# A two-layer streaming encoder step: the layer loop unrolled, the norms crossed in two groups of 280 tokens, more weight slots

## The reference

```python
def _rmsnorm(x, g):
    xf = x.astype(jnp.float32)
    y = xf * lax.rsqrt(jnp.mean(xf * xf, axis=-1, keepdims=True) + EPS)
    return (y * g.astype(jnp.float32)).astype(x.dtype)
...
    h = _rmsnorm(x, p['g_pre_mix'])
    (qn, qr, ckv, kr, qb, kb, vb, qc, kc, vc, alr, gc, gate) = _split_cols(h @ p['w_in'])
    # A: latent attention, B: sliding-window attention, C: gated linear attention
...
def _merge(oa, ob, oc, gate, p):
    g = jax.nn.sigmoid(gate).reshape(gate.shape[:-1] + (N_BRANCH, D_MODEL))
    y = (g[..., 0, :] * (oa @ p['w_up_a']) + g[..., 1, :] * (ob @ p['w_up_b'])
         + g[..., 2, :] * (oc @ p['w_up_c']))
    return y @ p['w_out']

def _residual(x, mix, p):
    x = x + _rmsnorm(mix, p['g_post_mix'])
    f = jnp.square(jax.nn.relu(_rmsnorm(x, p['g_pre_mlp']) @ p['w_ff1'])) @ p['w_ff2']
    return x + _rmsnorm(f, p['g_post_mlp'])
```

## Time and profile before

| | |
|---|---|
| median of three runs | 2607.6 us |
| profiled execution | 2612.26 us |
| its span, first to last instruction | 2610.5 us |
| mean granted TensorE clock | 0.971 of full |
| busy: PE, PEld, POOL, DVE, ACT | 2465.8, 2280.5, 1123.3, 984.5, 943.5 us |
| loaded weight units | 305 of 512 KB |
| DMA | 189.45 MB, mean 73 GB/s |

### The profile page before, as it was taken

One profiled execution on the slowest core, in us unless ns is written; L12 is line 12 of the kernel. 1 busy time (PEld: TensorE's weight loads), 2 busy tenths in 40 slices (PEclk: granted clock), 3 DMA queues, 4 the chain that ended last, 5 costly groups with the idle time before them and its releaser, 6 DMA issues.

```text
span 2610.5 us, 42794 instructions
## 1 busy us (share of the span) xinstructions
PE 2465.8 (94%) x17996; PEld 2280.5 (87%) x17996; DVE 984.5 (38%) x1746; ACT 943.5 (36%) x1757; POOL 1123.3 (43%) x677
## 2 busy tenths in 40 slices
PE   7999999999999799999879999999999997999997
PEld 6999878798798799999779998878977997999996
DVE  4566435435622411111355555444256124111113
ACT  4344423332444432322334443333333544322322
POOL 5433223333355464544343432233334455645543
PEclk8999999999999899999989999999999998999998
DMA  4111311121123122222121114111211231222222
GB/s 149 56 63 55 105 54 49 45 69 56 41 73 116 42 88 89 82 89 82 64 81 57 62 56 118 41 49 47 75 49 41 81 108 49 82 89 86 85 90 84
DMA packets 57464, 189.45 MB, mean 73 GB/s; under 512 B 8048, under 2 KB 12880, under 8 KB 56624
## 3 DMA queue, kind: packets, MB, share of 16 engines
q1 hardware_dynamic: 47120, 165.90, 19.5%
q10 hardware_dynamic: 10144, 20.73, 2.5%
HBM read 172.44 MB, written 10.89 MB: 70 GB/s over the span
## 4 chain that ended last, share of the span: by engine, by line
PE 44%; DVE 3%; POOL 2%; ACT 1%; issue 1%; DVEq 0%; POOLq 0%
PE dense L695 35%; PE att L743 1%; PE att L930 1%; PE att L991 1%; DVE h_raw L1530 1%; PE att L881 1%; PE att L820 1%; POOL h_lo L1860 1%; PE att L806 0%; POOL wlo L1855 0%; DVE x L1513 0%; PE att L947 0%; PE att L964 0%; PE att L824 0%; PE att L997 0%
## 5 line engine op out<-in xcount | busy, mean ns | idle before, releaser
L1855 POOL TENSOR_TENSOR wlo<-wraw,whi 128x1024 fp32r<-128x1024 f32 x298 | 715.4, 2402 | 947.5 <-ACT whi L1060 947.5
L695 PE MATMUL dense<-h_hi,whi 128*128 128x280 f32 x3200 | 947.4, 296 | 17.5 <-ACT cproj L1098 8.3
L695 PE MATMUL dense<-h_lo,whi 128*128 128x280 f32 x3200 | 938.8, 293 | 0.0
L695 PE MATMUL dense<-h_hi,wlo 128*128 128x280 f32 x3200 | 936.6, 293 | 0.0
L695 PEld LDWEIGHTS dense<-h_hi,whi 128*128 128x128 f32 x3200 | 607.5, 190 | 41.3 <-issue 16.4
L695 PEld LDWEIGHTS dense<-h_hi,wlo 128*128 128x128 f32 x3200 | 606.4, 189 | 1.5 <-issue 0.8
L695 PEld LDWEIGHTS dense<-h_lo,whi 128*128 128x128 f32 x3200 | 607.0, 190 | 0.0
L1060 ACT ACTIVATE whi<-wraw 128x1024 fp32r<-128x1024 f32 x298 | 312.5, 1049 | 294.6 <-DMA wraw<-in_w 256.0
L695 PE MATMUL dense<-hid_lo,whi 128*128 128x280 f32 x1024 | 298.4, 291 | 0.0
L695 PE MATMUL dense<-hid_hi,whi 128*128 128x280 f32 x1024 | 297.8, 291 | 0.0
L695 PE MATMUL dense<-hid_hi,wlo 128*128 128x280 f32 x1024 | 297.6, 291 | 0.0
(11 more groups left out here) (290 smaller groups left out, 3619.5 us busy)
## 6 DMA issues: line engine op xcount, KB each, us to landing
wraw<-in_w SPq DMA_DIRECT2D x305, 512.0 KB, 3.4
x_spill<-x ACTq DMA_DIRECT2D x2, 2240.0 KB, 7.9
x<-x_spill ACTq DMA_DIRECT2D x2, 2240.0 KB, 9.2
k_cat<-k_rope ACTq DMA_DIRECT2D x16, 212.0 KB, 3.5
x<-in_x SPq DMA_DIRECT2D x4, 560.0 KB, 5.4
out_y_out<-x SPq DMA_DIRECT2D x1, 2240.0 KB, 7.3
out_c_out<-ckv ACTq DMA_DIRECT2D x2, 560.0 KB, 6.6
const<-in_const SPq DMA_DIRECT2D x1, 1112.0 KB, 10.9
```

The costliest lines, as they stand in the source:

```text
L695: mm = pe.matmul(bank[0:m, 0:HALF], a[:, k, o * 128:o * 128 + m], b[:, k, H[hf]], start=(k == 0 and i == 0), stop=(k == kt - 1 and i == 2))
L1855: pool.tensor_tensor(wlo[slot][:, :], wraw[slot][:, :], whi[slot][:, :].bitcast(F32), ALU.subtract).then_inc(pool_done, st.done("pool", f" ...
```

## The change

The two layers are written out one after the other, in one block, with steps marked by their layer; parameters of both are loaded once. x comes in four DMAs, halves of the tokens, and y leaves in four. A new step `("half", u, hf)` does one half of a unit. `lap` builds each crossing: the last `LAP` = 5 units ahead of a norm are done for tokens 0 to 279 first; under their second halves the first half of the tokens is normed; the first five units after the norm are done for these tokens, and under them the second half is normed. There are 13 weight slots in place of three, most of them on space that is free only in some stages (`slots_for`), and `w` steps split each unit as soon as its slot's last user is done and its load can have come. Dense results of `out`, `ff1`, `ff2` and the first five units of a layer rotate over six PSUM banks. The squares of x are now added up by DVE, and TensorE only multiplies the sum. y is split two tiles at a time, after each `up_b` unit, into the tiles of `oc`. The level masks are made after the first half units, and the three tiles of head 0 are cleared after the scans; the first level products wait for the evacuation of the first five units. In the last layer no `next` norm is formed.

```diff
 WSLOTS = 3
+LAP = 5
...
+        BASE, MLP, MIX, EDGE = range(0, 3), range(3, 5), range(5, 9), range(9, 13)
+        w_at = r_w + [work + 24 * row + 8192 * i for i in range(2)] + [work + 8192 * i for i in range(4)] + [r_oc + 8192 * i for i in range(4)]
...
-        sq = at("sq", [P, KD, T], F32, r_oc + KD * row)
-        sqsum, sqpart = sq[:, 0, :], [sq[:, 1, :], sq[:, 2, :]]
+        mix = at("mix", [P, KD, T], F32, work + 16 * row)
         facc = at("facc", [P, KD, T], F32, work + 16 * row)
+        nsum = at("nsum", [P, 4, T], F32, work + 24 * row + 2 * 8192)
...
+        DENSE_BANKS = [dps[0][:, 0:HALF], dps[1][:, 0:HALF]] + [ps[:, b, 0:HALF] for b in (T0, T1, M_, O_)]
...
+            U_MIX, V_MLP = [UIDX["out", n] for n in range(KD - LAP, KD)], [UIDX["ff1", n] for n in range(LAP)]
+            U_MLP, V_NEXT = [UIDX["ff2", 32 - LAP + n] for n in range(LAP)], list(range(LAP))
...
+            def lap(l, post, pre, first, second):
+                for hf, (at_l, units) in enumerate((first, second)):
+                    for i, u in enumerate(units):
+                        plan.append((at_l, ("half", u, 1 - hf)))
+                        if i == 0:
+                            plan.extend([(l, ("ms", post, hf)), (l, ("norm", post, hf))])
+                        if i == LAP - 2:
+                            plan.extend([(l, ("ms", pre, hf)), (l, ("tokens", pre, hf))])
...
+                order.append(("half", 0, 1))
+                gla_steps((0, "p z"), (0, "v decay"), (0, "v arg 0"))
+                for u in V_NEXT[1:]:
+                    order.append(("half", u, 1))
+                    if UNITS[u][0] == "cq":
+                        gla_steps((0, "v arg 1"))
+                    if UNITS[u][0] == "ck":
+                        gla_steps((0, "v lev 0"), (0, "v arg 2"), (0, "v lev 1"), (0, "v end"), (0, "v lev 2"))
+                gla_steps((0, "p lev 0"), (0, "v kend"), (0, "v amat 0"), (0, "v amat 1"), (0, "v amat 2"))
                 dense()
-                if h > 0:
-                    gla_steps((h - 1, "p o"), (h - 1, "v o"))
-                gla_steps((h, "v arg 1"))
+                gla_steps((0, "p lev 1"), (0, "p ktok"), (0, "v amat 3"), (0, "v amat 4"), (0, "v ktok"))
                 dense()
-                if h > 0:
...
+                for u in range(next(dn), NU):
+                    kind, n = UNITS[u]
+                    if u in V_MLP:
+                        continue
+                    plan.append((l, ("half" if u in U_MIX + U_MLP else "dense", u) + ((0,) if u in U_MIX + U_MLP else ())))
+                    if kind == "up_b":
+                        plan.append((l, ("split_y", n)))
+                    if u == U_MIX[-1]:
+                        lap(l, "post_mix", "pre_mlp", (l, U_MIX), (l, V_MLP))
+                        plan.extend([(l, ("half", v, 1)) for v in V_MLP])
+                if l + 1 < DEPTH:
+                    lap(l, "post_mlp", "next", (l, U_MLP), (l + 1, V_NEXT))
+                    plan.append((l, ("spill",)))
+                else:
+                    for i, u in enumerate(U_MLP):
+                        plan.append((l, ("half", u, 1)))
+                        if i == 0:
+                            plan.extend([(l, ("ms", "post_mlp", 0)), (l, ("norm", "post_mlp", 0))])
+                    plan.extend([(l, ("ms", "post_mlp", 1)), (l, ("norm", "post_mlp", 1))])
+            plan += [(-1, ("square", 0)), (0, ("w", 0)), (-1, ("ms", "next", 0)), (-1, ("tokens", "next", 0)), (0, ("w", 1)),
+                     (-1, ("square", 1)), (0, ("half", 0, 0)), (0, ("w", 2)), (-1, ("ms", "next", 1)), (-1, ("tokens", "next", 1)),
+                     (0, ("half", 1, 0)), (-1, ("spill",)), (0, ("w", 3)), (0, ("half", 2, 0)), (0, ("w", 4)), (0, ("half", 3, 0)), (-1, ("masks",)), (0, ("half", 4, 0))]
+            for l_ in range(DEPTH):
+                layer_plan(l_)
...
+            def slots_for(l, u):
+                kind, n = UNITS[u]
+                if kind in ("out", "ff1", "ff2"):
+                    if kind == "out" or (kind == "ff1" and n < 8):
+                        return [*MLP, *MIX] if u in U_MIX else [*BASE, *MIX] if u in V_MLP else [*BASE] if kind == "out" else [*BASE, *MLP]
+                    if kind == "ff2" and n >= 24:
+                        return [*MLP, *EDGE] if u in U_MLP else [*BASE]
+                    return [*BASE, *MLP]
+                return [*BASE, *EDGE] if u in V_NEXT else [*BASE]
...
+                b = min(SIX if wide else TWO, key=lambda c: bank_free[c])
+                bank_of[key] = DENSE_BANKS[b]
+                before[key] = bank_user[b]
+                if kind in ("out",) and b > 1 and bank_user[b] is not None and bank_user[b][0] != l_:
...
+                ys = io["y_out"].rearrange("(k p) t -> p k t", p=P)
+                for hf in range(2):
+                    for g in range(2):
+                        for e, k in (("dve", 4 * g + 2), ("pool", 4 * g + 3)):
+                            sp.wait_ge(by_name[e], A(e, f"x post_mlp {k} {hf}", DEPTH - 1))
+                        sp.dma_start(ys[:, 4 * g:4 * g + 4, H[hf]], x[:, 4 * g:4 * g + 4, H[hf]]).then_inc(last_stored, 16)
+                sp.wait_ge(last_stored, 64)
...
+                def mean_square(which, hf):
+                    part = 0 if which.startswith("post") else 1
+                    pe.wait_ge(dve_done, A("dve", f"sum {which} 7 {hf}"))
+                    if l < 0 and hf == 0:
+                        pe.wait_ge(ones_loaded, 32)
+                    mm = pe.matmul(ps[:, S0 + hf, 0:HALF], c_("ones_d"), nsum[:, part, H[hf]], start=True, stop=True)
+                    mm.then_inc(pe_done, st.done("pe", f"ms {which} {hf}"))
...
+                        if h == 0:
+                            for u in V_NEXT:
+                                e = evac_engine(UNITS[u][0])
+                                pe.wait_ge(by_name[e], A(e, f"evac {u} 0 1"))
...
+                def square_x(which, hf, ready):
                     for k in range(KD):
+                        ready(k)
+                        if k >= 3:
+                            act.wait_ge(dve_done, A("dve", f"sum {which} {k - 2} {hf}"))
+                        dst = nsum[:, 1, H[hf]] if k == 0 else nsum[:, 3, H[k % 2]]
+                        act.activation(dst, x[:, k, H[hf]], ACT.Square).then_inc(act_done, st.done("act", f"sq {which} {k} {hf}"))
...
+                        for k in (step[1], step[1] + 1):
                             e = y_engine("b", k)
-                            round_tile(h_hi[:, k, :], y[:, k, :], (by_name[e], A(e, f"y b {k}")), f"y hi {k}")
-                        if step[1] == 1:
+                            round_tile(oc_hi[:, k, :], y[:, k, :], (by_name[e], A(e, f"y b {k}")), f"y hi {k}")
...
+                        if pre and k >= 3:
+                            add_square_x(pre, k - 2, hf)
+                    if pre:
+                        add_square_x(pre, KD - 2, hf)
+                        add_square_x(pre, KD - 1, hf)
...
+                    if s == "v arg 0" and h == 0:
+                        pool.wait_ge(dve_done, A("dve", "gla scan 0"))
...
-        with nc.Fori(0, DEPTH) as l:
-            with nc.Block() as block:
-                layer(l, block)
-            for s_ in block_sems:
-                nc.sync.sem_clear(s_)
-            nc.all_engine_barrier()
```

More of the change, by code:

```diff
@@ L485, in dense @@
[L485 to L498 removed]
+            plan = []
+            U_MIX, V_MLP = [UIDX["out", n] for n in range(KD - LAP, KD)], [UIDX["ff1", n] for n in range(LAP)]
@@ L564, in layer @@
-            order += [("norm", "post_mlp"), ("mean", "next")]
-            JOBS = {"a": jobs, "b": jobs_b}
+                gla_steps((last, "v out"))
+                order.append(("prep_a", 0))
+                for steps in ((1, 2), (3, 4, 5), (10, 11), (6, 7), (8, 9, 12, 13)):
+                    dense()
+                    if steps[0] == 1:
+                        gla_steps((last, "v oc"))
+                    order.extend([("prep_a", s) for s in steps])
+                for j in range(len(JOBS["a"]) + 2):
+                    order.append(("att", "a", j))
+                    if j not in (5, 10, 15, 21):
+                        dense()
@@ new lines, in program @@
+            loads = {}
+            for l_ in range(DEPTH):
+                for u in range(NU):
+                    n_ = sum(slot_of[k] == slot_of[l_, u] for k in loads)
+                    loads[l_, u] = 16 * (n_ + 1)
+            guard_of = {}
+            for l_ in range(DEPTH):
+                for u in range(NU):
+                    kind, n = UNITS[u]
+                    if kind in ("out", "ff1") and slot_of[l_, u] in [*MLP, *MIX]:
+                        guard_of[l_, u] = (l_, UIDX["up_b", 6])
+                    if slot_of[l_, u] in EDGE and (l_ > 0 or u > LAP):
+                        guard_of[l_, u] = (l_, UIDX["ff2", 23]) if u > LAP else (l_ - 1, UIDX["ff2", 23])
@@ new lines, in program @@
```

(14 more changed lines are left out.)

759 lines of the change are left out of this document (379 added, 380 removed).

## The result

The changed kernel took 2589.98 us (median of four runs, 2583.6 to 2591.78) against 2607.31 us before: a ratio of 0.9931, 95% interval 0.9913 to 0.9949. It is faster by 17 us, and the forecast was 49 us. The direction held; the size did not, and the time is that of the second rival. The profiled execution took 2590.14 us, span 2588.4, 22.1 us less than the profiled one before.

The account below looks back on a forecast made before the run. TensorE, busy 94% of the span, was taken as the bound, so only its idle or slow-clock time could be won. Terms summed to 48.9 us off 2607.6: 2558.7, say 2559 us, range 2533 to 2588.

Parts of the forecast that it names:

- the second rival: Waits move into head 0 and the crossings' second halves: crossings lose 27 us, head 0 costs 20; 2590 us, chance 0.18.
- I take 2.2 us for it: Slow clock behind the 11.9 us wait before head 0's level products; part of head 0's -14 us for two layers.
- 19.2, and 1.5: Loss per MLP norm crossing, 19.2 us plus 1.5 for slow clock, against 29.6 before; 17.6 us won for two.
- I get the end of unit 0 at 40.7: Kernel start: unit 0 ends at 40.7 us with four further half units done; 4.6 us won.
- The boundary: Between the layers: the same crossing in halves loses 19.9 us in place of 37.1; 17.2 us won.
- the y split: Before the output projection: y split in pairs after each up_b unit leaves about 0.6 us lost; 12 us won.
- the end: Kernel end: norm of the first half under the last half units, 17.4 us against 31.9; 14.5 us won.
- Head 1's -3: Linear attention, head 1: three units of cover instead of four, 1.5 us of standing in each layer; 3 us lost.

## Why the prediction was wrong

Its list of places was complete, and its direction right in six of the seven terms. Three steps failed in size, the third in its sign too, and they hold 34 us between them (9.7, 12.6 and 11.8):

1. **"I take 2.2 us for it"** (the clock behind head 0's wait). I had priced it from a window behind 1.7 us of idle time; behind 12 us it costs 6.8 and 5.7 us, as the run with the filled wait measures. The wait itself was forecast well, 11.9 against 12.39 and 11.04, and so was its cause; in the chain of layer 1 the clearing, the split between the differences and DVE's slow operation beside it are all there. The term is -23.7 and not -14.
2. **The crossings: "19.2, and 1.5"**. The first half came out as worked out (first wait 2.9 said, 2.31 measured; first half unit of ff1 done after 26 us, and after 26). In the second half the chain is some 6 us longer: I had the evacuations of `ff1` and the splits in it, but each alone; a square beside a split takes 2.2 to 2.4 us for 0.44, and ACT waits for it, in order, ahead of both rstd. The run with the other order takes 7.6 and 6.2 us out, and so shows that ACT's order is a step of it; the slow square is read from the timeline alone. It doesn't show all: 18.7 and 21.7 us stay lost, about the 20.7 that I had forecast for the order as it was. With layer 1's weaker crossing the two gave 5 us and not 17.6.
3. **"I get the end of unit 0 at 40.7"** (start). The split of unit 3 stands behind the second half's tokens in the queue, and that of unit 1 beside the sums. I had laid GpSimd's work end to end, without the waits for ACT between: 53.15 is 12 us late, and the run with the other order takes 8.2 of them back.

The boundary (15.0 for 17.2), the y split (13 for 12) and the end (17 for 14.5) were right within 3 us. For the y split and the start a run shows the cause; for the boundary the unrolled kernel shows part of it; the end is only read from the two traces.

Head 1's -3 became -4.7, and for another reason than its queues: a wait of 1.52 us lowered the clock in layer 0 and not in layer 1. The number near the forecast is luck. The same wait stands ahead of head 1 in both layers of all twelve profiled executions of the changed kernel and its variants: in 10 of the 24 places the level products and the unit behind them took 16.1 us, in 14 they took 11.4. So each of the two places can add 4.8 us to an execution whatever was changed, and differences of this size between two medians or two traces must be read place by place. The remaining +8 is of the same kind: in the kernel before the clock was 0.91 over 20 us in three windows of layer 1 (behind 1420, 1480 and 1540 us) and in one of each layer's second attention (behind 590 and 1890), where the changed kernel has 1.00, with waits as long (1.3 and 0.7 us) except at the first, where it has none; each gives 1.5 to 1.7 us. I don't know what decides which of these short waits the clock follows. The four executions of the changed kernel lie 8 us apart (2583.6 to 2591.78 us, mean clock 0.971 to 0.965).

Rival 2 named 2590 us, with 20 us lost in head 0 (measured 19.5 and 18.6) and 27 in a crossing (26.3, 27.9). Its chance of 0.18 was too low: I had bounded the clock only from the nearest row, and the paced chains only from operations that stand alone. The range ended at 2588 although the rival's own time was 2590. That the rival met the time within a microsecond is luck in part: it had 27 us lost at the boundary too, where 22.1 were, and it had neither the start's 12 us nor the 8 us of clock.

## What to carry to other kernels

Where TensorE is the bound, a wait that is put ahead of it costs its length and then a stretch at half the clock; price both, and look for one more unit of work to put there before shortening the chain. Overlapping two groups of tokens moves the bound to the in-order engines: here the order on ACT was worth 6 to 8 us in an MLP crossing (and cost 2.9 at the boundary), one unit more of overlap 0 to 2.7. And when a list of work beside a fixed pattern is shifted by one, other kinds of unit meet the tight places; here that was worth more (28 us in the two attentions) than the whole change (17), and it is tried in a line.

## What the runs showed of the hardware

- Behind 12.39 us of idle time TensorE ran at 0.50 for the 48 level products (9.8 us for 5.3) and recovered only in the next unit; with the wait filled by products that nobody reads the clock stayed at 1.00. A page of the Trainium skill (TensorE: Matmul & The Clock Gate, A second HAM failure mode) tells of short idle times between groups of products that make the clock swing; in the latent attention this case's trace agrees: 0.73 + 2.11 us of idle time and 0.81 over the next 18 us, against 0.92 us and 1.00. Behind the wait of 1.52 us ahead of head 1 the clock fell in 10 of 24 cases.
- DVE's squares and level products, of 256 or 280 columns with two inputs, took 0.42 to 0.45 us alone, but 2.2 to 2.6 us when they started within half a microsecond after GpSimd's split of 2.4 us did; they then ended 0.3 us behind it (885.89 to 888.10 against 885.41 to 887.80). Where the split started into a row of DVE's level products (head 1, 137.56), they kept their 0.44 us each and the split took 4.28. The Trainium skill (SBUF — State Buffer, Terms) says that one of the two holds their shared ports for its whole instruction and the other stands; the durations agree, in both directions.
- Of the 12.35 us at the loop's end 4.3 went with the loop; 8.07 stayed with the block's end, the clearing of the semaphores and the engines' meeting.
